# A hybrid decoder layer on one core: x laid out turned, the first norm's factors applied behind the input products, the first block with k outermost

## The reference, cut to what matters

```python
proj = rmsnorm(h, norm_mix_g) @ w_in            # 512x1024 @ 1024x4624, h = x
y_a  = gmlp_chunk_mixer(proj[..., :2048])       # GELU, norm of v, mixing in chunks of 128 tokens
y_b  = ssd_mixer(proj[..., 2048:])              # conv + SiLU of xBC, softplus of dt, scan in chunks, SiLU gate
h    = h + concat(y_a, y_b) @ w_out
hid  = relu(rmsnorm(h) @ w_ff1);  h = h + (hid * hid) @ w_ff2
gate = sigmoid(rmsnorm(h) @ w_ple_gate);  h = h + gate * (p @ w_ple_proj)
return rmsnorm(h, final_norm_g)
# rmsnorm(x, g) = x * rsqrt(mean(x*x) + 1e-6) * g, the mean over the 1024 of one token
```

## Time and profile before

| | us |
|---|---|
| time, median of 3 runs | 733.08 (733.01 to 733.64) |
| span of the profiled execution | 731.3 |
| its own time | not measured apart; the runs are 1.7 to 2.3 above its span |
| PE busy | 721.8 (99%) |
| DVE busy | 528.3 (72%) |
| ACT busy | 410.3 (56%) |
| POOL busy | 134.1 (18%) |

### The profile page before, as it was taken

One profiled execution on the slowest core, in us unless ns is written; L12 is line 12 of the kernel. 1 busy time (PEld: TensorE's weight loads), 2 busy tenths in 40 slices (PEclk: granted clock), 3 DMA queues, 4 the chain that ended last, 5 costly groups with the idle time before them and its releaser, 6 DMA issues.

```text
span 731.3 us, 9961 instructions
## 1 busy us (share of the span) xinstructions
PE 721.8 (99%) x3962; PEld 622.3 (85%) x3962; DVE 528.3 (72%) x552; ACT 410.3 (56%) x521; POOL 134.1 (18%) x112
## 2 busy tenths in 40 slices
PE   8999999999999999999999999999999999999996
PEld 7888887778887888888899889988999889988884
DVE  5556795477658555555889985899579967898874
ACT  6534456653576762413767742774447625673875
POOL 1021000756645000001110211212111121020000
PEclk9999999999999999999999999999999999999998
DMA  8632222343233153219667898889978997887311
GB/s 330 205 105 86 87 87 89 115 151 109 86 111 120 60 201 116 73 43 285 151 170 211 178 296 159 218 192 295 206 180 222 221 250 156 235 177 260 115 58 58
DMA packets 52229, 118.24 MB, mean 162 GB/s; under 512 B 5052, under 2 KB 5208, under 8 KB 52184
## 3 DMA queue, kind: packets, MB, share of 16 engines
q1 hardware_dynamic: 39816, 84.03, 34.4%
q0 software_dynamic: 11136, 29.36, 22.1%
q10 hardware_dynamic: 1232, 4.23, 1.8%
HBM read 96.60 MB, written 4.23 MB: 138 GB/s over the span
## 4 chain that ended last, share of the span: by engine, by line
PE 97%; DMA 1%; DVE 1%; ACT 1%; issue 0%; SPq 0%
PE acc L1651 28%; PE acc L1653 28%; PE acc L1652 28%; PE side L1716 3%; PE side L1651 2%; PE side L1652 2%; PE side L1653 2%; PE side L1809 2%; PE side L1776 1%; DMA w_raw<-in_w_in 1%; PE side L1816 1%; PE side L1804 1%; DVE w_lo L1108 0%; PE side L1756 0%; PE side L1757 0%; PE side L1796 0%
## 5 line engine op out<-in xcount | busy, mean ns | idle before, releaser
L767 ACT ACTIVATE ring_hi<-quarter 128x1024 fp32r<-128x1024 f32 x112 | 113.6, 1051 | 101.9 <-PE acc L1653 46.5
L1409 DVE TENSOR_TENSOR ring_lo<-quarter,ring_hi 128x1024 fp32r<-128x1024 f32 x112 | 132.8, 1219 | 38.0 <-ACT ring_hi L767 37.7
L1651 PE MATMUL acc<-w_hi,a_hi 128*128 128x512 f32 x256 | 104.4, 408 | 0.1
L1653 PE MATMUL acc<-w_hi,a_lo 128*128 128x512 f32 x256 | 100.1, 391 | 0.0
L1652 PE MATMUL acc<-w_lo,a_hi 128*128 128x512 f32 x256 | 99.8, 390 | 0.0
L648 POOL DMA_DIRECT2D quarter<-in_w_ff x24 | 29.2, 1236 | 240.4 <-DMA quarter<-in_w_ff 240.2
L1652 PE MATMUL acc<-xS_lo,ring_hi 128*128 128x256 f32 x256 | 72.4, 283 | 0.0
L1108 DVE TENSOR_TENSOR w_lo<-w_raw,w_hi 128x1024 fp32r<-128x1024 f32 x36 | 48.0, 1336 | 27.1 <-ACT w_hi L669 26.7
L1651 PEld LDWEIGHTS acc<-w_hi,a_hi 128*128 128x128 f32 x256 | 48.1, 188 | 11.5 <-issue 1.4
L1652 PEld LDWEIGHTS acc<-w_lo,a_hi 128*128 128x128 f32 x256 | 48.2, 188 | 10.7 <-issue 1.4
L1653 PEld LDWEIGHTS acc<-w_hi,a_lo 128*128 128x128 f32 x256 | 48.0, 188 | 10.4
(11 more groups left out here) (290 smaller groups left out, 1817.7 us busy)
## 6 DMA issues: line engine op xcount, KB each, us to landing
quarter<-in_w_ff SPq DMA_DIRECT2D x72, 512.0 KB, 5.8
w_raw<-in_w_in SPq DMA_DIRECT2D x36, 512.0 KB, 3.7
quarter<-quarter POOLq DMA_DIRECT2D x32, 512.0 KB, 8.0
quarter<-in_w_ff POOLq DMA_DIRECT2D x24, 512.0 KB, 7.4
w_raw<-in_w_out SPq DMA_DIRECT2D x16, 512.0 KB, 3.5
h<-in_x SPq DMA_DIRECT2D x8, 512.0 KB, 4.7
seg<-cs_dram ACTq DMA_DIRECT2D x8, 512.0 KB, 3.8
w_raw<-in_w_ple_gate SPq DMA_DIRECT2D x8, 512.0 KB, 5.7
```

The source lines that it names most:

```text
L767: act.activation(ring[n % 3][0][at], quarter[i][at], ACT.Copy).then_inc(form_hi, 1)
L1409: dve.tensor_tensor(lo[at], src, hi[at].bitcast(F32), ALU.subtract).then_inc(form_lo, 1)
L1651: pe.matmul(dst, st[0], mv[0], start=start, stop=False)
L1653: return pe.matmul(dst, st[1], mv[0], start=False, stop=stop)
```

## The change

- The host hands in x a second time, turned (`x_turned`, 1024 x 512), and `norm_mix_g` as a 128 x 8 array. SP loads the k tiles of the turned x into `y`, alternately with the k tiles of block 0's weights (256 KB each, sixteen in all), then the four token tiles of x, then block 1's weights. ACT itself issues the small load of g.
- ACT and DVE split each k tile of the turned x, times g (now one number for each partition), straight into `a_hi` and `a_lo`, and each k tile of block 0's weights. PE neither turns x nor waits for the norm. `first_block` runs block 0 with k outermost: for each k tile the products of all four token tiles, in four banks.
- The factor of the tokens is applied behind the products: as the `scale` of GELU and SiLU in the blocks with tokens on the partitions. For the convolution's groups it is made a row: four diagonal matrices, one product with `ones` behind group 4 (`rstd_row`), a copy by ACT. DVE multiplies each convolution group by it from the bank into `tmp`, which frees the bank; ACT and DVE go on from `tmp`. The copy of `dt` out of its bank is such a multiplication too, by DVE, and ACT adds the bias behind it.
- The four `sums` and block 1's splits stand behind the first block's splits. The reductions of v's squares and the new multiplication stand first in DVE's turn, before the copies of `cs` and `csT` and before `split_lo`.
- `ones` is set by DVE, the warm-up uses it alone: 11 products, and none of the nine later ones. SP loads the gain of the second norm behind block 8's weights.

```diff
-WARM = 14
-REWARM = 9
+WARM = 11
@@ SP
+            for k in range(KT):
+                sp.dma_start(xt_raw[:, k, :], xt_dram[:, k, :]).then_inc(xt_landed[k], 16)
+                sp.dma_start(w_raw[:, k // 2, k % 2, :], w_in[:, k, W:W + 512]).then_inc(first_landed[k], 16)
+            for s in range(NS):
+                load_x(s)
             load_k(V + 1, w_in, W + 512)
...
-            sp.wait_ge(xn_ready, NS)
-            load_gain(a["norm_mlp_g"][0], 0)
             load_k(U, w_in, 0)
...
+            sp.wait_ge(dve_evac, 4 * (U - X))
+            wait_free(sp, "dt")
+            load_gain(a["norm_mlp_g"][0], 0)
@@ ACT
+            act.dma_start(g_col[:], a["norm_mix_g"]).then_inc(g_col_landed, 16)
             act.wait_ge(eps_ready, 1)
             act.activation(early_rms[:], eps[:], ACT.Sqrt).then_inc(sqrt_loaded, 1)
+            act.wait_ge(g_col_landed, 16)
+            for k in range(KT):
+                split_xt(k)
+                split_first(k)
+            for s in range(NS):
+                sums(0, s)
+            for p in range(4):
+                split_hi(1, p)
+            act.wait_ge(rstd_ready, NS)
...
+                if t == 6:
+                    freed(act.activation(rstd_row, wait_full(act, "rstd_row"), ACT.Copy), "rstd_row")
...
                 if t == 11:
-                    bank = wait_full(act, "dt")
+                    wait_free(act, "dt")
                     act.wait_ge(small_landed, 16 * 4)
-                    ins = act.activation(dtT[:], bank[0:2 * R, :], ACT.Identity, bias=dt_b[:])
-                    freed(ins, "dt")
+                    act.activation(dtT[:], dtT[:], ACT.Identity, bias=dt_b[:]).then_inc(dt_biased, 1)
...
-                    act.activation(h[:, s, 512 * b:512 * b + 512], acc[:, s, :], ACT.Gelu).then_inc(act_evac, 1)
+                    act.activation(h[:, s, 512 * b:512 * b + 512], acc[:, s, :], ACT.Gelu, scale=rstd[:, s:s + 1]
+                                   ).then_inc(act_evac, 1)
                 elif b < U:
...
-                    act.activation(conv[:, i % 2, :], acc[:, s, :], ACT.Copy, scale=cols[:, 36 + i:37 + i]
+                    act.wait_ge(*emptied(b, s))
+                    act.activation(conv[:, i % 2, :], tmp[:, i % 2, :], ACT.Copy, scale=cols[:, 36 + i:37 + i]
                                    ).then_inc(conv_begun, 1)
-                    act.wait_ge(*emptied(b, s))
+                    act.wait_ge(conv_step, 3 * i + 3)
@@ DVE
+            dve.memset(ones[:], 1.0).then_inc(ones_ready, 1)
             dve.memset(eps[:], EPS).then_inc(eps_ready, 1)
+            dve.wait_ge(g_col_landed, 16)
+            for k in range(KT):
+                split_xt(k)
+                split_first(k)
+            dve.wait_ge(consts_ready, 2)
+            for s in range(NS):
+                dve.wait_ge(rms_ready, s + 1)
+                dve.reciprocal(rstd[:, s:s + 1], rms[:, s:s + 1]).then_inc(rstd_ready, 1)
+                dve.wait_ge(rstd_ready, s + 1)
+                dve.tensor_scalar(rstd_diag[:, s, :], ident[:], rstd[:, s:s + 1], None, ALU.mult
+                                  ).then_inc(diag_ready, 1)
+            for p in range(4):
+                split_lo(1, p)
...
             for t in range(4 * OUT):
                 b, s = divmod(t, 4)
+                if 5 <= t < 9:
+                    i = t - 5
+                    dve.wait_ge(v_sq, i + 1)
...
+                if t == 11:
+                    bank = wait_full(dve, "dt")
+                    freed(dve.tensor_tensor(dtT[:], bank[0:2 * R, :], rstd_row[0:2 * R, :], ALU.mult), "dt")
+                if X <= b < U:
+                    i = t - 4 * X
+                    dve.wait_ge(acc_full, t + 1)
+                    if i == 0:
+                        dve.wait_ge(v_sum, NS)
+                        wait_free(dve, "rstd_row")
+                    if i >= 2:
+                        dve.wait_ge(conv_begun, i - 1)
+                        dve.wait_ge(conv_step, 3 * (i - 1))
+                    dve.tensor_tensor(tmp[:, i % 2, :], acc[:, s, :], rstd_row, ALU.mult).then_inc(dve_evac, 1)
                 if t == 16:
                     bank = wait_full(dve, "decay")
                     dve.tensor_copy(cs[:], bank[:, 0:NS * R]).then_inc(cs_ready, 1)
...
-                split_lo(b + 1, s)
+                if b:
+                    split_lo(b + 1, s)
...
-                        ins = dve.scalar_tensor_tensor(dst, acc[:, s, 0:SEQ - k], w, dst, ALU.mult, ALU.add)
+                        dve.scalar_tensor_tensor(dst, tmp[:, i % 2, 0:SEQ - k], w, dst, ALU.mult, ALU.add
+                                                 ).then_inc(conv_step, 1)
@@ PE
+            def first_block():
+                for k in range(KT):
+                    pe.wait_ge(xa_lo, k + 1)
+                    if k % 2:
+                        pe.wait_ge(lo_ready, k // 2 + 1)
+                    else:
+                        pe.wait_ge(first_lo, k // 2 + 1)
+                    for s in range(NS):
+                        at = (slice(None), k, slice(s * P, s * P + P))
+                        ins = product(acc[:, s, :], [t[at] for t in (a_hi, a_lo)],
+                                      [t[:, 0, k, :] for t in (w_hi, w_lo)], k == 0, k == KT - 1)
...
-            pe.wait_ge(consts_ready, 3)
+            pe.wait_ge(ones_ready, 1)
             for i in range(WARM):
-                pe.matmul(acc[:, i % 2, 0:P], ident[:], ones[:], start=True, stop=True)
-            turn_norm(0, 0)
-            for i in range(REWARM):
-                pe.matmul(acc[:, i % 2, 0:P], ident[:], ones[:], start=True, stop=True)
+                pe.matmul(acc[:, i % 2, 0:P], ones[:], ones[:], start=True, stop=True)
+            first_block()
+            pe.wait_ge(consts_ready, 2)
...
+                if t == 4:
+                    bank = open_bank("rstd_row")
+                    pe.wait_ge(diag_ready, NS)
+                    filled(pe.matmul(bank, ones[:], rstd_diag.rearrange("p s n -> p (s n)"), start=True, stop=True),
+                           "rstd_row")
```

More of the change, by code:

```diff
@@ L220, in build_layer @@
         xt_hi = sem("xt_hi")
+        xt_landed = [sem(f"xt_landed{i}") for i in range(KT)]
+        first_landed = [sem(f"first_landed{i}") for i in range(KT)]
+        g_col_landed = sem("g_col_landed")
+        xa_hi, xa_lo = sem("xa_hi"), sem("xa_lo")
+        first_hi, first_lo = sem("first_hi"), sem("first_lo")
+        diag_ready = sem("diag_ready")
+        dt_biased = sem("dt_biased")
+        ones_ready = sem("ones_ready")
         consts_ready = sem("consts_ready")
@@ L290, in last_user @@
             return b - 1, (2 + s // 2 if prev else s)
-        plan = [(("xt", 0, s, q), (2 * s + q) % 4) for s in range(NS) for q in range(2)]
-        plan += [("cols", 2)]
+        plan = [("cols", 2), ("rstd_row", 3)]
         for t in range(9, 20):
@@ L413, in lo_count @@
             return 7 * u + LO_ORDER.index(name) + 1
+        xt_raw = y[:].rearrange("p s (a n) -> p (s a) n", a=2)
+        rstd_diag = conv[:, 1, :].rearrange("p (s n) -> p s n", s=NS)
+        rstd_row = gain[:, 0, 0:SEQ]
         block = ctx.enter_context(nc.Block())
@@ L420, in piece @@
             def piece(b, p, src, dst, shift=0):
-                if not (isinstance(b, int) and b == 0):
-                    sp.wait_ge(lo_ready, 4 * (b - 1) + p + 1 + shift)
+                sp.wait_ge(lo_ready, 4 * (b - 1) + p + 1 + shift)
                 sp.dma_start(dst, src).then_inc(w_landed[p], 16)
@@ L571, in _ @@
             pool.memset(ident[:], 0.0).then_inc(consts_ready, 1)
-            pool.memset(ones[:], 1.0).then_inc(consts_ready, 1)
-            pool.wait_ge(consts_ready, 2)
+            pool.wait_ge(consts_ready, 1)
             pool.affine_select(out=ident[:], in_=ident[:], compare_op=ALU.not_equal, fill=1.0, base=0,
                                pattern=[[-1, P]], channel_multiplier=1).then_inc(consts_ready, 1)
+            pool.wait_ge(ones_ready, 1)
             pool.affine_select(out=upper[:], in_=ones[:], compare_op=ALU.is_ge, fill=0.0, base=0,
@@ L704, in sums, with split_xt, split_first, xt_evac @@
                                ).then_inc(rms_ready, 1)
-            def xt_evac(n, s):
-                hi = a_hi if n == 0 else g_hi
+            def split_xt(k):
+                act.wait_ge(xt_landed[k], 16)
+                act.activation(a_hi[:, k, :], xt_raw[:, k, :], ACT.Copy, scale=g_col[:, k:k + 1]).then_inc(xa_hi, 1)
+            def split_first(k):
+                act.wait_ge(first_landed[k], 16)
+                act.activation(w_hi[:, 0, k, :], w_raw[:, k // 2, k % 2, :], ACT.Copy
+                               ).then_inc(hi_ready if k % 2 else first_hi, 1)
+            def xt_evac(s):
                 for q in range(2):
-                    bank = wait_full(act, ("xt", n, s, q))
-                    c = s if n < 2 else TILES[s]
-                    act.activation(hi[:, 4 * q:4 * q + 4, c * P:c * P + P],
```

(35 more changed lines are left out.)

119 lines of the change are left out of this document (39 added, 80 removed).

## The result

The changed kernel takes 745.0 us (743.08 to 745.83, 4 runs) against 733.05 before (732.97 to 733.64): a ratio of 1.0158, 95% interval 1.0143 to 1.0172, so 12 us slower. The forecast was 733.4. The traced execution is the longest of the four (745.83); its span is 744.1 us, 12.8 more than before.

A forecast was written before the change was run, and what follows sets the result against it. TensorE, busy 721.8 of 731.3 us, bounds the kernel. A 7.3 us gain up to group 7 against 7.65 us of convolution waits gives +0.35; with 1.8 outside the span, 733.4 us, range 730.7 to 736.5.

The forecast's parts named there:

- The start: Beginning of block 0: warm-up from about 1.1 to 5.8, first product at 5.9 us instead of 10.99.
- The handover: Block 0 to block 1: PE waits 0.3 us for group 0's GELU, ends 0 and 3.3; last weight piece landed at 24.9.
- rival A: Slower: block 1's last weight piece lands late and delays the handover, 3.3 us instead of 0.3, 736.4; chance 0.15.
- the stretch to group 7: Start until group 7 is full: at 50.9 instead of 58.25 us, a gain of 7.3.
- Groups 12 to 15: Convolution: DVE's multiplication and low half delay SiLU, PE waits behind groups 13 to 15; +2.3 us for the stretch.
- B: Faster: the waits of groups 12 to 14 do not come, only those of 16 and 17; 731.1 us; chance 0.15.
- Group 17: `csT` copied 0.95 us after the full group, then 2.7 of ACT work before PE's next `mix` product: +3.85 us.
- C: Faster: none of the queue waits reaches PE; 725.8 us; chance 0.10.
- Group 16: `cs` copied after the full group, then ACT's exponential with its table load hidden; PE waits: +1.5 us.
- Group 18 to the scan: Forecast 0: ACT runs about 1 us later against PE from group 20 on, taken up by its idle time.
- D: Slower: first k tile comes as late as the first weight piece did, PE begins at 8; 735.5 us; chance 0.05.
- E: Slower: ACT's lag behind group 19 comes out in the scan, 1 to 2 us; 734.9 us; chance 0.07.

The follow-up runs named there:

- late-copies kernel: Kernel before the change, with only DVE waiting for the full group before copying `cs` and `csT` in turns 16 and 17: 740.47 us.
- From PSUM: Changed kernel, with the multiplication writing back into the PSUM bank and ACT and DVE reading the bank, DVE's order kept: 740.82 us.
- throwaway products: Changed kernel plus 14 throwaway products of 128 columns on PE behind group 16: 743.47 us.
- kernel with copies first and PSUM: Changed kernel, with the `cs` and `csT` copies before the multiplication and the multiplication in the PSUM bank, low half still behind it: 729.73 us.
- the best one: Changed kernel with early copies, multiplication in PSUM, `dt` operations before turn 12's multiplication, and group 0's GELU before block 1's last high half: 727.59 us.
- both with copies and PSUM: Two changed kernels with early `cs`/`csT` copies and the multiplication in PSUM: low half behind it 729.73 us, low half ahead of it 733.7 us.
- the one without the row factor: Changed kernel without multiplying the convolution groups by the tokens' factors, the row still made, ACT and DVE reading the bank: 728.34 us.

## Why the prediction was wrong

- **The start** held: first product 6.05 (5.9), released by DVE's first low half. The new warm-up ran from 1.12 to 5.40, 4.28 us, less than 22 x 0.213 = 4.7: the fast pitch of the earlier trace rows came before its end, at about 4.3 instead of 6.4. In the eight traces with this warm-up the same 22 instructions, all from 1.12 on, took 4.07 to 5.06 us, so that moment is not fixed; the first product moved only between 6.01 and 6.29.
- **The handover** was mis-sized: 1.1 us of wait, 0.3 forecast. The last weight piece let ACT start at 26.10, not 24.9. This is rival A's mechanism, at a quarter of its price. With 0.15 from the start it makes 0.95 of the 1.3 us that the stretch to group 7 fell short of the forecast; the rest is spread.
- **Groups 12 to 15** held in sum: 2.0 (2.3), with waits of 1.0, 0.2 and 0.2. B falls.
- **Group 17** held: 4.0 (3.85). C falls.
- **Group 16**: the step "the table load before the exponential is hidden, since ACT would be through with its other work by then" failed. The load does not run ahead of a wait for `cs` that stands before it, idle ACT or not:

```profile
114.01 1.28 ACT L889 ACT_TABLE_LOAD   x1 [2.44 <-DVE cs L1306]
```

  It makes the wait 2.7 instead of 1.5 (1.3 and the 0.2 of run-ahead). The sum had, besides, no term for the clock, 1.7 us behind that wait in this trace. The late-copies kernel shows both, the load behind the wait and the half clock, without any of the change's other work: the order of DVE's queue alone costs 7.3 us there, and taking it back gave 8.7 in the changed kernel. The clock's term is not a fixed one: the traces of *From PSUM* and of the throwaway products have it behind group 17 and not here.
- **Group 18 to the scan**, 7.4 us, the largest miss: the step "From group 20 on ACT runs about 1 us later against PE than before; its idle time takes that up" failed, because the sum gave DVE's terms the 2.31 us of the earlier trace rows whether they read PSUM or SBUF. Moved to `tmp`, they have two SBUF inputs, and beside POOL they took 5.8; the low half ahead of them took 2.22 instead of 1.22. The SiLU of group 18 began 8.6 us behind the full bank (145.18) where it had been 3.1 (135.21), so 5.5 later and not 1. ACT's evacuations and the `b_nat` copy came late behind it; PE waited 4.4 us, and then worked for 6.0 us (148.63 to 154.6) at half clock, worth 3.0. The trace before held the warning: the low half takes 2.08 us while POOL squares v, and 1.22 elsewhere, and the three terms from PSUM took 2.31 with POOL at work.

```profile
42.61 1.89 POOL L592 TENSOR_TENSOR tmp<-h 128x1024 f32<-128x1024 f32 x1 [38.62 <-ACT h L916]
...
43.51 2.08 DVE L1108 TENSOR_TENSOR w_lo<-w_raw,w_hi 128x1024 fp32r<-128x1024 f32 x1 [3.74 <-ACT w_hi L669]
```

```profile
132.86 2.31 DVE L1345 SCALAR_TENSOR_TENSOR conv<-acc,cols,conv 128x511 f32<-128x511 f32 x3 [1.92 <-ACT conv L923]
...
133.62 2.40 POOL L604 TENSOR_TENSOR seg<-seg,upper 128x1024 f32<-128x1024 f32 x1
```

  I read neither against the moved operand.

  The Trainium skill (GPSIMD Engine Reference, 1. Specifications) says that GpSimd shares its SBUF interfaces with VectorE and contends with DVE instructions that have two SBUF inputs. By that rule this trace agrees: 5.78 us with two, 2.31 with one. It is the rule that spoke against this change, and it was not weighed.
- **The other rivals.** D falls (first product 6.05). E had the right place, ACT's lag behind group 19, but put it at 1 to 2 us where it was 7.4, and without its cause, the slow terms.
- **Open:** the stretch behind the scan's first product, 585.4 us before and 586.3 after, with short waits of PE for DVE's splits in the feed-forward part. The kernel with copies first and PSUM has 728.0 - 142.59 = 585.4 there, the best one 726.1 - 140.26 = 585.8. The other traces have 585.4 to 586.0, so most of the 0.9 us may be no more than the spread. No run was made for it.

## What to carry to other kernels

An operation put at the head of an in-order queue, with a wait for the newest result, holds back everything behind it until that result is there; ask of each thing behind it who needs it, before asking what the new operation costs. When an operand moves from PSUM to SBUF, look up what the other engines do at that time, not only how long the operation took. A wait of the bounding engine can cost its clock too (here 1.6 to 3.1 us on top of waits of 1.5 to 4.4), or not, so its price is a range. A short independent operation right behind the head (here the weights' low half) is worth keeping there as cover for the other engine's step.

## What the runs showed of the hardware

- Three DVE operations of 511 columns with one PSUM and one SBUF input take 2.31 us with POOL busy beside them; with two SBUF inputs they take 2.31 us with POOL idle, and 5.78 and 6.64 beside POOL. A 1024-column subtraction with two SBUF inputs goes from 1.22 to as much as 2.69 beside POOL.
- A table load of 1.28 us runs ahead of its instruction's wait in some places (53.88 in the changed kernel, its square root waits until 56.17) and stands behind a wait in another: that for `cs`, at 114.01 in the changed kernel and 117.27 in the one with late copies. What decides it, no run shows.
- The granted clock fell to one half in or behind PE waits of 1.5 us (*From PSUM*, the handover), 2.1, 2.7, 3.7, 4.3 and 4.4 us, for 3.4 to 6.8 us each time. It stayed at 1.00 behind others of 2.4 (throwaway products, group 19), 2.7, 3.1 (late copies, group 17) and 3.7. In the five traces whose waits behind the start stay at or under 1.4 us (the kernel before, both with copies and PSUM, the one without the row factor, the best) it reads 1.00 up to 690 us.
